# Writing out the remaining engine loops of a two-layer RWKV-7 and sparse-attention decoder

## What is computed

```python
x = x + 0.5 * swiglu(rmsnorm(x, norm_ffn1[l]), ffn1_w_gate[l], ffn1_w_up[l], ffn1_w_down[l])   # 1024 -> 2816 -> 1024
h = rmsnorm(x, norm_mix[l])
x = x + rwkv7_time_mix(h, ...)      # layer 0: 16 heads of 64, a recurrence over the tokens
x = x + nsa_attention(h, shared, w_q, q_norm, w_o)   # layer 1: 16 heads of 64
x = x + 0.5 * swiglu(rmsnorm(x, norm_ffn2[l]), ...)
```

## Time and profile before

| what | value |
|---|---|
| median of three runs | 2701.41 us (2699.93 to 2706.42) |
| the profiled execution, own time | 2708.74 us |
| its span, first to last instruction | 2706.9 us |
| mean granted TensorE clock | 0.948 of 2.4 GHz |
| PE busy | 2434.5 us, 90%, 16952 matmuls |
| DVE busy | 1606.1 us, 59% |
| ACT busy | 634.9 us, 23% |
| POOL busy | 563.5 us, 21% |
| HBM | 79 GB/s over the span |

### The profile page before, as it was taken

The page is one execution under the profiler, slowest core; times in us unless marked ns, Lnnn a source line. Parts: engine busy times, 40 slices in busy tenths (PEclk is TensorE's granted clock), DMA queues, the critical chain, the costliest instruction groups (busy, mean ns, idle before and its releaser), DMA issues. The chain is left out here.

```text
span 2706.9 us, 44357 instructions
## 1 busy us (share of the span) xinstructions
PE 2434.5 (90%) x16952; PEld 1977.2 (73%) x16952; DVE 1606.1 (59%) x2182; ACT 634.9 (23%) x1246; POOL 563.5 (21%) x382
## 2 busy tenths in 40 slices
PE   7999977987888869999999699999849898999998
PEld 6888865765666657888877588888638687788887
DVE  6646569945666545656556465656536565565654
ACT  3100012223545322101012310101435453210001
POOL 3212135421212102302030021213111300221213
PEclk9999997998999979999999799999969899999999
DMA  4333222430000012333325333332351101333331
GB/s 133 103 94 101 82 74 71 128 110 29 16 30 16 17 33 78 96 99 101 94 78 163 106 101 94 93 99 73 113 130 37 37 2 32 94 103 91 103 87 66
DMA packets 375943, 216.95 MB, mean 80 GB/s; under 512 B 18880, under 2 KB 359808, under 8 KB 375776
## 3 DMA queue, kind: packets, MB, share of 16 engines
q1 hardware_dynamic: 367648, 198.83, 26.0%
q10 hardware_dynamic: 8128, 15.83, 1.6%
HBM read 198.73 MB, written 15.89 MB: 79 GB/s over the span
## 5 line engine op out<-in xcount | busy, mean ns | idle before, releaser
L143 DVE TENSOR_TENSOR w_lo_ffn<-w_raw,w_hi_ffn 128x1024 fp32r<-128x1024 f32 x272 | 508.7, 1870 | 9.4
L387 POOL TENSOR_TENSOR act_ffn<-gated_ffn,usc_ffn 128x512 f32<-128x512 f32 x88 | 128.1, 1456 | 1007.4 <-ACT gated_ffn L367 1007.4
L367 ACT ACTIVATE gated_ffn<-gsc_ffn 128x512 f32<-128x512 f32 x88 | 55.8, 634 | 1010.4 <-DVE gsc_ffn L292 1010.4
L150 PE MATMUL p_gate_ffn<-hhi_ffn,w_hi_ffn 128*128 128x512 f32 x704 | 278.2, 395 | 7.6 <-DVE hlo_ffn L205 7.6
L150 PE MATMUL p_up_ffn<-hhi_ffn,w_hi_ffn 128*128 128x512 f32 x704 | 274.6, 390 | 2.9 <-DVE w_lo_ffn L143 2.9
L151 PE MATMUL p_gate_ffn<-hlo_ffn,w_hi_ffn 128*128 128x512 f32 x704 | 277.2, 394 | 0.0
L150 PE MATMUL p_down_ffn<-ahi_ffn,w_hi_ffn 128*128 128x512 f32 x704 | 274.9, 390 | 2.4 <-DVE x_res L303 2.4
L152 PE MATMUL p_gate_ffn<-hhi_ffn,w_lo_ffn 128*128 128x512 f32 x704 | 276.9, 393 | 0.0
L292 DVE TENSOR_TENSOR gsc_ffn<-p_gate_ffn,rstd_ffn 128x512 f32<-128x512 f32 x88 | 60.9, 692 | 363.6 <-PE p_up_ffn L152 363.0
L151 PE MATMUL p_up_ffn<-hlo_ffn,w_hi_ffn 128*128 128x512 f32 x704 | 274.6, 390 | 0.0
L152 PE MATMUL p_up_ffn<-hhi_ffn,w_lo_ffn 128*128 128x512 f32 x704 | 274.5, 390 | 0.0
(11 more groups left out here) (341 smaller groups left out, 4490.5 us busy)
## 6 DMA issues: line engine op xcount, KB each, us to landing
w_raw<-in_ffn_w_gate_dram SPq DMA_DIRECT2D x88, 512.0 KB, 3.8
w_raw<-in_ffn_w_up_dram SPq DMA_DIRECT2D x88, 512.0 KB, 3.8
w_raw<-in_ffn_w_down_dram SPq DMA_DIRECT2D x64, 512.0 KB, 4.1
w_raw<-in_ffn_w_down_dram SPq DMA_DIRECT2D x32, 384.0 KB, 3.4
w_raw<-in_rw_w_rkv_dram SPq DMA_DIRECT2D x24, 512.0 KB, 4.5
rkv_scratch<-staged_mix ACTq DMA_DIRECT2D x24, 256.0 KB, 2.5
w_raw<-in_kv_w_dram SPq DMA_DIRECT2D x12, 512.0 KB, 4.7
w_raw<-in_rw_w_o_dram SPq DMA_DIRECT2D x8, 512.0 KB, 5.4
```

The lines of the kernel that those rows point to most:

```text
L143: nc.vector.tensor_tensor(lo, raw, fp(hi), ALU.subtract).then_inc(s["w_ready"], 1)
L150: nc.tensor.matmul(out, whi, hi, start=first, stop=False)
L367: nc.scalar.activation(gated[:], gsc[:, j], ACT.Silu).then_inc(s["silu"], 1)
L387: nc.gpsimd.tensor_tensor(act32[:], gated[:], usc[:, j], ALU.mult).then_inc(s["act32"], 1)
```

## The change

Every `Fori` loop that was left becomes a Python loop, so that each trip is written out with `i` a plain number; waits and addresses become constants. The `ready` increments and waits go, and the semaphore goes from the lists of ffn and mix_project (attention's list keeps it, unused). The order of the instructions on each engine stays. The diff, cut to its core (the same edit at SP, DVE, ACT and POOL where it says so):

```diff
@@ ffn: SP, and in the same way DVE, ACT, POOL
-                with sp.Fori(0, nf // 2 - skip) as i:
+                for i in range(nf // 2 - skip):
...
-                with sp.Fori(0, ND // 4) as i:
+                for i in range(ND // 4):
@@ ffn: PE
-                    with pe.Fori(0, nf // 2 - 1) as i:
+                    for i in range(nf // 2 - 1):
                         gate_up(i + 1, False)
                 else:
-                    with pe.Fori(0, nf // 2) as i:
+                    for i in range(nf // 2):
                         gate_up(i, False)
@@ ffn: ACT, and in the same way POOL
-                        act.sem_inc(s["ready"], 1)
@@ mix_project: all engines
             elif name in MAIN:
-                with eng.Fori(0, n // 4) as i:
+                for i in range(n // 4):
                     for j in range(4):
                         body(4 * i + (base + j), (base + j) % 4, i + (base + j) // 4, 4 * i + j, j)
@@ mix_project: DVE, ACT, POOL
-            dve.sem_inc(s["ready"], 1)
...
-                act.wait_ge(s["ready"], 1)
...
-                pool.wait_ge(s["ready"], 1)
@@ project_add: PE
-            with pe.Fori(0, ND // 4) as i:
+            for i in range(ND // 4):
@@ attention: SP, PE, ACT, DVE
-            with sp.Fori(0, 2) as i:
+            for i in range(2):
...
-            with pe.Fori(0, 2) as i:
+            for i in range(2):
...
-                    act.sem_inc(s["ready"], 1)
...
-            with act.Fori(0, 2) as i:
+            for i in range(2):
...
-            with dve.Fori(0, 2) as i:
+            for i in range(2):
```

More of the change, by code:

```diff
@@ L224 @@
 FFN_SEMS = ["raw0", "raw1", "raw2", "raw3", "w_free", "w_hi", "w_ready", "gate", "gu_free", "x_done", "a_lo", "a_hi",
-            "act32", "silu", "sq", "sq_sum", "ready"] + NORM_SEMS
+            "act32", "silu", "sq", "sq_sum"] + NORM_SEMS
 def ffn_first_units(w_gate, w_up):
@@ L285, in _ @@
             for f0, nf in groups:
-                with dve.Fori(0, nf // 2) as i:
+                for i in range(nf // 2):
                     for j in range(2):
@@ L361, in _ @@
             for f0, nf in groups:
-                with act.Fori(0, nf // 2) as i:
+                for i in range(nf // 2):
                     for j in range(2):
@@ L380, in _ @@
             for f0, nf in groups:
-                with pool.Fori(0, nf // 2) as i:
+                for i in range(nf // 2):
                     for j in range(2):
@@ L388, in _ @@
                         pool.wait_ge(s["a_hi"], f + 1)
-                        pool.sem_inc(s["ready"], 1)
                         nc.gpsimd.tensor_tensor(flat(alo[:, one(2 * i + j)]), act32[:], flat(fp(ahi[:, one(2 * i + j)])),
@@ L403 @@
 MIX_SEMS = ["raw0", "raw1", "raw2", "raw3", "w_free", "w_hi", "w_ready", "rstd", "h", "ms_mm", "ms",
-            "dx", "mix32", "mix_hi", "mix_lo", "out", "st0", "st1", "st2", "st3", "ready", "pad"]
+            "dx", "mix32", "mix_hi", "mix_lo", "out", "st0", "st1", "st2", "st3", "pad"]
 def mix_project(core, tag, rkv, lora):
```

## The result

The changed kernel is slower: median 2714.31 us over 15 runs (2705.81 to 2721.78) against 2705.76 (2698.99 to 2706.95), ratio 1.0036, 95% interval 1.0024 to 1.0048. The forecast was 2687.3, range 2677 to 2697. The profiled execution of the changed kernel took 2706.30 us (span 2704.5), near the short end of its spread, so its totals flatter it; the stages are what to read.

A forecast was written before the change was run, and what follows sets the result against it. PE was taken to bound the feed-forward stages, and a chain hopping between engines attention. Gains of 8.5 + 3.3 + 1.5 + 0.5 + 0.3 = 14.1 us off the median 2701.4 gave 2687.3, range 2677 to 2697.

The forecast's parts named there:

- Term 1: Attention, where its two trips meet: without the jump the stalls for issue go, 8.5 us gained.
- Rival A: Attention's edge and hops: ACT's second stall stays and shorter hops are swallowed; gain only 6.7 us, 2694.7; chance 0.16.
- rival B: Behind attention's edge: TensorE's clock stays up or returns at once, 5 us more gain, 2682; chance 0.12.
- Terms 2 and 4: Attention: shorter hops between engines within it, 3.3 us; earlier query load at its start, 0.5 us.
- Term 3: The k pass of mix_project: DVE's weight splitting, which PE waits for, gets faster; 1.5 us gained.
- Term 5: The rest: two starts of project_add and five semaphores less to clear, 0.3 us gained.
- Term 6: Feed-forward loops: no gain, since PE does not wait at their edges and covers the other engines' costs.
- rival C: PE's new written-out code arrives late, mainly in feed-forward stages: 21 more packets cost 62 us, 2749; chance 0.05.
- The nine unexplained waits: PE's weight loads at one line of the recurrence: 26.4 us, up to 5.0, taken as possibly late code.

The follow-up runs named there:

- the padded ones: Kernels with increments of an unused semaphore added on PE; in the changed kernel's first feed-forward stage 145, 209 and 81 gave ratios 0.9970, 1.0022 and 0.9970.
- all but attention: The changed kernel with the two-trip loops of attention put back: 2719.02 us, ratio 1.0060 to the kernel before.

## Why the prediction was wrong, point by point

**Term 1, the edge: right.** The place in the changed kernel:

```profile
2146.98 0.89 PE L1749 MATMUL bank_att<-ident,osb_att 128*128 128x128 f32 x4 [0.79 <-DVE osb_att L1940]
...
2147.80 1.91 PE L1727 MATMUL bank_att<-kc_att,qp_att 64*128 64x31 f32 x8
2147.91 0.60 ACT L1829 ACTIVATE o_hi<-bank_att 128x512 fp32r<-128x512 f32 x1 [4.15 <-PE bank_att L1749]
...
2148.54 0.69 DVE L1900 TENSOR_TENSOR o_lo<-bank_att,o_hi 128x512 fp32r<-128x512 f32 x1 [1.70 <-ACT o_hi L1829]
...
2149.75 0.29 DVE L1886 TENSOR_TENSOR masked_att<-bank_att,cmp_neg_att 128x124 f32<-128x124 f32 x1 [0.52 <-PE bank_att L1727]
...
2151.92 1.03 PE L1753 MATMUL bank_att<-ident,probs_att 128*31 128x128 f32 x4 [0.90 <-ACT probs_att L1812]
```

All the "issue" stalls of the earlier trace rows are gone, ACT's second one too. From the turn to the first transposed probabilities it is 2151.92 - 2146.98 = 4.94 us, where it was 2153.93 - 2140.28 = 13.65: 8.7 us, forecast 8.5. Rival A fell with it. So did rival B: in the changed kernel too TensorE stood at half speed behind the edge.

```profile
2154.00:2158.00 4.00, 4.00 (x17) 3.05 (x15) 1.50 (x6) 1.19 (x5) 0.00 (x0) 0.50 1.07 208
```

**Terms 2 and 4, hops and start of attention: a size too large.** The hops did get shorter: at the edge L1900 starts 0.03 behind the end of L1829, and PE's wait for `o_lo` is down from 7.8 to 6.3.

```profile
PE bank_att L1759 <- DVE o_lo L1900: 6.3, 6, 1.1
```

DVE's first load wait is 10.3 instead of 11.76. But little of it reached the end. The second turn came 2087.68 - 1998.2 = 89.5 us after the stage's start, and in the changed kernel 89.6:

```profile
2094.88 0.59 ACT L1829 ACTIVATE o_hi<-bank_att 128x512 fp32r<-128x512 f32 x1
```

Of 3.3 + 0.5 us some 1.3 came (10.0 - 8.7), most of it behind the edge: the first trip took 142.1 us before (2140.28 - 1998.2) and 141.7 now. This is the part of rival A that held, that the hops are swallowed; its reason, that a PE that comes sooner waits longer, fits but was not tested by itself. By stage means attention gave 8.9, hardly more than the edge.

**Term 3, the k pass: right.** L488 (before L492) now stands 0.72 behind L484:

```profile
512.65 0.68 DVE L484 TENSOR_TENSOR sq_sum<-h_mix 128x512 f32<-128x512 f32 x1
513.37 0.75 DVE L488 SCALAR_TENSOR_TENSOR mix_mix<-sq_sum,vecs,h_mix 128x512 f32<-128x512 f32 x1
```

and mix_project is 1.3 us shorter in every profile, forecast 1.5.

**Term 5 can't be told** from the scatter of the small stages (project_add behind the recurrence took 55.0 to 56.5 in either form).

**Term 6, the feed-forward loops: right for their own stages.** The first one is 374.8 to 375.1 in all the profiles, and the later ones differ by at most 1.6 us from profile to profile, whichever form they have.

**The step that failed** is the sentence below term 6: nothing is reordered, no wait is added, each queue issues the same DMAs. With it the sum put the recurrence at nothing. It became 14.5 us longer (412.3 against 397.8 in the mean), more than the 10.2 that attention and mixing gave. One queue did not issue the same: the instruction queue. I had seen it as rival C and given it 5%. I argued that the new code is in stages where 192 instructions last over 20 us, many times longer than in the recurrence, and that the written-out code there has no such wait. That is so, and beside the point. I took the cost of code as packets times a price, 21 extra at some rate, so that it had to fall where the extra packets are. It falls on packets that were always there. The nine unexplained waits of the earlier trace rows that I priced it by have little to do with it: they are about as long in every placement (26.4 before, 25.0 to 28.4 in the padded ones). The stage and the price were wrong, and the count (134 forecast, 135 came) was right by luck. I had divided all 33904 instructions by 113 packets, though a loop's packets serve several trips; a packet holds 256. So the 6336 new ones are 24.75 packets and not 21, and all but attention has indeed 137, 24 more than before. Attention written out took 3 fewer (110), which I had not counted; the two errors cancel.

## What to carry to other kernels

Writing out a loop changes the page boundaries of all the code behind it. Straight-line code whose instructions are very short (here 256 in 2 us) pays for a boundary in the wrong place; code of long instructions does not. So before you take "no line of that stage changed" as proof that it costs the same, compare its length, look for "issue" waits that return at one line, and try an unrolling with a few dozen empty instructions of padding in an idle place of the same engine: here two of three amounts turned a loss of 0.36% into a gain of 0.30%.

## What the runs showed that I had not expected

- PE got a page of 256 instructions every 3.47 us at best, though it issued one in 1.95. At the stop shown it went on only 1.4 us after the packet had landed.
- The places where PE stopped could be computed to the instruction from the padding; which of them hurt could not, since it also depends on when the next packet starts.
- An increment of a semaphore on PE took 0.15 us, not the 0.05 that I had expected: 145 of them ran from 0.80 to 22.95 us, and PE's first matmul of setup came at 23.06 us instead of 9.72. The same 145 cost nothing between matmuls that PE's sequencer had run ahead of.
- A stop of 1 to 2 us can be followed by 10 us at half the clock, in code that otherwise keeps 1.00; the same code, executed again, may keep it.
